# Seven block products in place of eight for the retention values and the first gate of a float32 two-layer kernel, with two of the weight sums made by adding DMAs

## The reference

```python
u = rmsnorm(h, norm_mix[l])
proj = u @ w_in[l]                                   # 1024 -> 7168
q, k, v, g_ret, p, gates = jnp.split(proj, split_points, axis=-1)
q = rotary(...); k = rotary(...) * (RET_QK_DIM ** -0.5)
ret = retention(q, k, v)                             # chunks of 64, decays
ret = ret * lax.rsqrt(jnp.mean(ret * ret, axis=-1, keepdims=True) + NORM_EPS)
ret = ret.reshape(b, s, RET_V) * jax.nn.silu(g_ret)
pool_out = multiscale_pool(p, pool_w[l], pool_scale[l])
gate = jax.nn.sigmoid(gates.reshape(b, s, 2, D_MODEL) + gate_bias[l])
merged = gate[:, :, 0] * (ret @ w_ret_up[l]) + gate[:, :, 1] * (pool_out @ w_pool_up[l])
h = h + merged @ w_out[l]
```

## Time and profile before

| | |
|---|---|
| Median of 3 runs | 1193.36 us (1192.82 to 1193.5) |
| The profiled execution's own time | 1193.28 us |
| Its span in the trace | 1191.5 us |
| PE busy | 1182.7 us, 99% of the span |
| DVE busy | 914.9 us, 77% |
| ACT busy | 674.6 us, 57% |
| POOL busy | 165.2 us, 14% |
| Granted clock of TensorE | 0.999 of full speed |

### The profile page before, as it was taken

The page is one execution under the profiler, slowest core; times in us unless marked ns, Lnnn a source line. Parts: engine busy times, 40 slices in busy tenths (PEclk is TensorE's granted clock), DMA queues, the critical chain, the costliest instruction groups (busy, mean ns, idle before and its releaser), DMA issues.

```text
span 1191.5 us, 14697 instructions
## 1 busy us (share of the span) xinstructions
PE 1182.7 (99%) x5728; PEld 982.1 (82%) x5728; DVE 914.9 (77%) x1143; ACT 674.6 (57%) x814; POOL 165.2 (14%) x169
## 2 busy tenths in 40 slices
PE   9999999999999999999999999999999999999997
PEld 8777888888888888888888888888899888888886
DVE  7788798878778798877798878645567666988884
ACT  7775656666547666554565555545333545666652
POOL 2100132210200132210132120000000000222200
PEclk9999999999999999999999999999999999999999
DMA  9434565547333565556455555745544455555540
GB/s 341 175 132 157 184 243 185 183 175 279 121 136 112 206 216 178 188 195 218 156 193 186 201 212 185 281 171 206 192 161 168 151 177 176 188 206 180 188 177 35
DMA packets 32728, 220.91 MB, mean 185 GB/s; under 512 B 3761, under 2 KB 4273, under 8 KB 7058
## 3 DMA queue, kind: packets, MB, share of 16 engines
q1 hardware_dynamic: 32514, 219.77, 51.5%
q10 hardware_dynamic: 144, 0.20, 0.0%
HBM read 218.91 MB, written 1.05 MB: 185 GB/s over the span
## 4 chain that ended last, share of the span: by engine, by line
PE 99%; issue 0%; DVE 0%; ACT 0%; POOL 0%; POOLq 0%; DVEq 0%; ACTq 0%
PE ps L259 30%; PE ps L261 30%; PE ps L260 30%; PE ps L264 5%; PE ps L267 3%; DVE h L406 0%; DVE AR L2579 0%; DVE st L1812 0%; DVE AR L1830 0%; ACT AR L2570 0%; POOLq L134 0%; POOL st L395 0%; POOL state L1546 0%; ACT yh L1862 0%; DVE st L1817 0%
## 5 line engine op out<-in xcount | busy, mean ns | idle before, releaser
L218 DVE SCALAR_TENSOR_TENSOR wlo<-raw,whi 128x2048 fp32r<-128x2048 f32 x160 | 366.3, 2294 | 114.4 <-ACT whi L211 87.1
L211 ACT CAST whi<-raw 128x2048 fp32r<-128x2048 f32 x162 | 310.0, 1914 | 193.6 <-PE ps L261 192.3
L259 PE MATMUL ps<-whi,xh 128*128 128x512 f32 x1040 | 409.9, 394 | 0.0
L261 PE MATMUL ps<-whi,xl 128*128 128x512 f32 x1040 | 405.4, 390 | 0.0
L260 PE MATMUL ps<-wlo,xh 128*128 128x512 f32 x1040 | 405.2, 390 | 0.0
L259 PEld LDWEIGHTS ps<-whi,xh 128*128 128x128 f32 x1040 | 195.2, 188 | 45.5 <-issue 1.4
L261 PEld LDWEIGHTS ps<-whi,xl 128*128 128x128 f32 x1040 | 195.2, 188 | 41.8
L260 PEld LDWEIGHTS ps<-wlo,xh 128*128 128x128 f32 x1040 | 195.4, 188 | 38.4
L259 PE MATMUL ps<-whi,yh 128*128 128x512 f32 x344 | 138.0, 401 | 0.0
L261 PE MATMUL ps<-whi,yl 128*128 128x512 f32 x344 | 134.4, 391 | 0.0
L260 PE MATMUL ps<-wlo,yh 128*128 128x512 f32 x344 | 134.0, 389 | 0.0
(11 more groups left out here) (256 smaller groups left out, 1379.8 us busy)
## 6 DMA issues: line engine op xcount, KB each, us to landing
raw<-in_w SPq DMA_DIRECT2D x198, 1024.0 KB, 4.8
raw<-in_w SPq DMA_DIRECT2D x4, 512.0 KB, 7.7
h<-in_x SPq DMA_DIRECT2D x4, 256.0 KB, 4.7
raw<-in_w SPq DMA_DIRECT2D x4, 256.0 KB, 4.3
AR<-in_b_pw SPq DMA_DIRECT2D x1, 1024.0 KB, 4.9
AR<-in_gate_bias SPq DMA_DIRECT2D x1, 1024.0 KB, 6.8
AR<-in_dft SPq DMA_DIRECT2D x1, 864.0 KB, 7.5
AR<-in_rmask SPq DMA_DIRECT2D x1, 768.0 KB, 8.7
```

Source lines behind the costliest of these rows:

```text
L211: e.copy(whi[:, v % S, :], raw[:, v % R, :]).then_inc(*sig.up("hi", v))
L218: e.scalar_tensor_tensor(out=wlo[:, v % S, :], in0=raw[:, v % R, :], scalar=1.0, in1=whi[:, v % S, :].bitcast(F32), op0=ALU.mult, op1=ALU. ...
L259: e.matmul(o, ah, bh, start=start, stop=False, skip_group_check=skip)
L261: return e.matmul(o, al, bh, start=False, stop=stop, skip_group_check=skip)
```

## The change

- v and g0 are each made by **seven block products** (`tensor_product`, p = 0 to 6) of 12 matmuls instead of eight quarters. The blocks are the two token halves, the two input halves and the two column halves. Three products (0, 2, 5) take the tokens as they are; four (1, 3, 4, 6) take one of four **token sums** (`vector_token_sums`, then a cast into `SX` on ACT and a low part `SL` on DVE, 128 x 2048 each, made once and used by both groups). Products 0, 2 and 3 take a weight block as it is (b11, b21, b22), the others a **weight sum**: product 1 takes b11 + b12, product 4 that plus b22, product 5 that plus b21, product 6 b12 + b22. Each of the seven is a unit of its own for `hi` and `lo`, so each group has seven casts and seven low parts where there were four.
- The sums for products 4 and 5 are made by DVE (`vector_group_sum`). Those for products 1 and 6 are made by **DMAs that add** (`accum_op`), issued by GpSimd: SP loads b11 into `first_sum` (the place of the token sums, so after those are read) and GpSimd adds b12 from memory to it; and GpSimd adds b22 from memory to the loaded b12 in its raw slot.
- Products share banks: 0, 4 and 6 follow each other in one (ps4), 1 and 3 in another (ps5), 2 and 5 in a third. Between them ACT copies what is there (`scalar_part`) and DVE adds to it (`vector_part`), as no matmul starts these banks anew.
- The order: the whole group v stands where v0 stood; the group g0 where v1 stood, ahead of q0. g00 and g01 are gone from behind gr1. Products ru0 follow gr1 at once, with the turns of the second retention half before and inside them. The gate's bias and sigmoid move along (`vector_gate_sum`, `scalar_gate`).
- The norm of this stage writes float32 tokens (`x32`) on ACT, then casts them (one 128 x 512 instruction) and takes the low part by one 128 x 512 instruction on DVE (before: four of 128 x 128 each).
- `vector_ret_norm` computes both token halves' sums before it scales either, in other scratch space.
- Convolution: chunk 2 has a split buffer of its own (`third`, in `SL`), and the wait is gone.

```diff
+RET = {"p0": 2, "p1": 2, "g10": 2, "g11": 2, "pw": 1, "v": 7, "pu0": 2, "pu1": 2, "g0": 7, "q0": 2, "k0": 2,
+       "q1": 2, "k1": 2, "gr0": 2, "gr1": 2, "ru0": 2, "ru1": 2, "out": 4}
+GROUPS = ("v", "g0")
+ADDED = {"v": (1, 6), "g0": (1, 6)}
+GROUP_RAW = (1, None, 2, 0, 1, 2, 3)
...
+        def raw_ready(v):
+            if v in added_at:
+                return sig.at("added%d" % (v - added_at[v]), v)
+            return sig.at("summed", v) if v in sums_at else raw_loaded(v)
+
+        def raw_free(n):
+            return lo_at(users[n][-1])
...
-                elif c == 2:
-                    q.wait_ge(*banks.filled("conv", 1, 0))
...
+        def vector_group_sum(e, q, g, k):
...
+            elif k == 4:
+                q.wait_ge(*lo_at(v))
+                q.wait_ge(*raw_loaded(v + 3))
+                q.wait_ge(*raw_ready(v + 1))
+                d = e.tensor_tensor(b11, first_sum, b22, ALU.add)
+            else:
+                q.wait_ge(*lo_at(v + 2))
+                q.wait_ge(*sig.at("summed", v + 4))
+                d = e.tensor_tensor(b21, b21, b11, ALU.add)
+            d.then_inc(*sig.up("summed", v + k))
+
+        def tensor_product(e, q, g, p):
+            bx, bz, by = GBANK[g]
+            v = RU[g] + p
+            b, key = ((bx, "x"), (bz, "z"), (by, "y0"), (bz, None), (bx, None), (by, "y1"), (bx, None))[p]
+            if key:
+                banks.take(b, g, key)
+                q.wait_ge(*banks.room(g, key))
+            else:
+                q.wait_ge(*sig.at("part", g, {3: 1, 4: 0, 6: 2}[p]))
...
+            for k in range(4):
+                c = slice(512 * k, 512 * k + 512)
+                last = mm3(e, ps[b][:, :], ah[:, k, :], al[:, k, :], whi[:, v % S, c], wlo[:, v % S, c],
+                           k == 0 and key is not None, k == 3, skip=True)
...
+        def scalar_part(e, q, g, i):
+            bx, bz, _ = GBANK[g]
+            p, b, t, j = ((0, bx, 0, 0), (1, bz, 1, 1), (4, bx, 0, 1), (6, bx, 1, 0))[i]
...
+        def vector_part(e, q, g, i):
+            bx, bz, by = GBANK[g]
+            p, b, t, j, parts = ((2, by, 0, 0, (0,)), (3, bz, 0, 1, (2,)), (6, bx, 1, 1, (1, 3)), (5, by, 1, 0, (3,)))[i]
...
@@ tensor_ret
-            chunk(e, q, "v0", RU["v0"], x)
+            for p in range(7):
+                tensor_product(e, q, "v", p)
...
-            chunk(e, q, "v1", RU["v1"], x)
+            for p in range(7):
+                tensor_product(e, q, "g0", p)
...
-            chunk(e, q, "g01", RU["g01"], x)
...
+            turn_x(e, q, "ret", None, 0, 1, vn[:, 0, :], "y", sig.at("gated", 1, 0))
+            quarter(e, q, "ru0", RU["ru0"], 0, 0, 0, yh, yl, y_ret)
+            quarter(e, q, "ru0", RU["ru0"], 0, 1, 0, yh, yl, y_ret)
+            turn_x(e, q, "ret", None, 1, 1, vn[:, 1, :], "y", sig.at("gated", 1, 1))
...
+        def gpsimd_first_sum(e, q, g):
+            v = RU[g]
+            q.wait_ge(*sig.at("ld_first", g))
+            e.dma_start(first_sum, wst[raw_of[v + 6]], accum_op=ALU.add).then_inc(*sig.up("added1", v + 1, by=16))
+
+        def gpsimd_last_sum(e, q, g):
+            v = RU[g]
+            q.wait_ge(*sig.at("added1", v + 1))
+            q.wait_ge(*raw_loaded(v + 6))
+            e.dma_start(raw_at(v + 6), wst[raw_of[v + 3]], accum_op=ALU.add).then_inc(*sig.up("added6", v + 6, by=16))
...
+                if v == raw_of[RU["v"]] - 1 and "v" in ADDED:
+                    q.wait_ge(*sig.at("x_low", "sums"))
+                    load(first_sum, wst[raw_of[RU["v"]]], "ld_first", "v")
+                if v == raw_of[RU["pu0"]] and "g0" in ADDED:
+                    q.wait_ge(*lo_at(RU["v"] + 1))
+                    q.wait_ge(*sig.at("summed", RU["v"] + 4))
+                    load(first_sum, wst[raw_of[RU["g0"]]], "ld_first", "g0")
```

More of the change, by code:

```diff
@@ L356, in norm_half_act @@
             q.wait_ge(*banks.filled("x", name, t, half))
+            if name == "nm":
+                b = banks.of["x", name, t, half]
+                q.wait_ge(*sig.at("sums", "n1", FAST - 1))
+                q.wait_ge(*sig.at("turned_lo", "n1", FAST - 1))
+                for i in range(4):
+                    k = 4 * half + i
+                    last = e.activation(x32[:, t, k, :], ps[b][:, 128 * i:128 * i + 128], ACT.Copy, bias=0.0,
+                                        scale=parm(name, k))
+                last.then_inc(*banks.empty("x", name, t, half))
+                q.wait_ge(*banks.emptied("x", name, t, half))
+                if x_free:
+                    q.wait_ge(*x_free)
+                e.copy(xh[:, 4 * half:4 * half + 4, tcols(t)],
+                       x32[:, t, 4 * half:4 * half + 4, :]).then_inc(*sig.up("xh", name, t, half))
+                return
             if x_free:
@@ L673, in vector_mix @@
             v = ff_down(U[FF[f][0]], j)
-            b11, b12, b21, b22 = (raw[:, v % R, 512 * k:512 * k + 512] for k in range(4))
+            b11, b12, b21, b22 = (raw_at(v)[:, 512 * k:512 * k + 512] for k in range(4))
             t3 = mix[:, 1, :]
-            q.wait_ge(*sig.at("raw%d" % (v % R), v))
+            q.wait_ge(*raw_ready(v))
             if j:
@@ L687, in vector_mix_rest @@
             v = ff_down(U[FF[f][0]], j)
-            b12, b21, b22 = (raw[:, v % R, 512 * k:512 * k + 512] for k in range(1, 4))
+            b12, b21, b22 = (raw_at(v)[:, 512 * k:512 * k + 512] for k in range(1, 4))
             t2, t4 = mix[:, 0, :], mix[:, 2, :]
@@ new lines, in scalar_part @@
+        def scalar_part(e, q, g, i):
+            bx, bz, _ = GBANK[g]
+            p, b, t, j = ((0, bx, 0, 0), (1, bz, 1, 1), (4, bx, 0, 1), (6, bx, 1, 0))[i]
+            q.wait_ge(*sig.at("made", g, p))
+            q.wait_ge(*sig.at("summed", "minus"))
+            q.wait_ge(*banks.filled("pooled", 3))
+            e.activation(group_dst(g, t, j), ps[b][:, :], ACT.Copy, bias=0.0,
+                         scale=(minus if j else rstd)[:, t:t + 1]).then_inc(*sig.up("part", g, i))
+        def vector_part(e, q, g, i):
+            bx, bz, by = GBANK[g]
+            p, b, t, j, parts = ((2, by, 0, 0, (0,)), (3, bz, 0, 1, (2,)), (6, bx, 1, 1, (1, 3)), (5, by, 1, 0, (3,)))[i]
+            q.wait_ge(*sig.at("made", g, p))
+            for n in parts:
+                q.wait_ge(*sig.at("part", g, n))
+            d = group_dst(g, t, j)
+            e.scalar_tensor_tensor(out=d, in0=ps[b][:, :], scalar=(minus if j else rstd)[:, t:t + 1], in1=d, op0=ALU.mult,
+                                   op1=ALU.add).then_inc(*banks.empty(g, DONE[t, j]))
@@ L2125, in vector_gate @@
             key = f"g{which}{j}"
-            dst = merged if which else sig0
+            dst = merged
             q.wait_ge(*banks.filled(key, t))
@@ L2162, in scalar_pool_out, with vector_pool_out @@
                 a.then_inc(*sig.up("pool_hi", g))
-        def vector_pool_out(e, q):
-            for g in range(4):
+        def vector_pool_out(e, q, groups):
+            for g in groups:
                 q.wait_ge(*sig.at("pool_hi", g))
@@ L2501, in vector_ret @@
             vector_ret_norm(e, q, 0)
+            for t in range(2):
+                vector_ret_scale(e, q, 0, t)
             for t in range(2):
```

352 lines of the change are left out of this document (254 added, 98 removed).

## The result

The changed kernel takes 1196.71 us (median of 7 runs, 1195.78 to 1197.29) where the kernel before takes 1193.43 (1192.82 to 1194.11): a ratio of 1.0028, 95% interval 1.0019 to 1.0037. It is slower by 3.3 us, inside the range and on the other side of no change than was forecast.

The account below looks back on a forecast made before the run. PE was taken as the bound, busy 1182.7 of 1191.5 us. Terms -5.45 - 0.2 + 0.8 + 1.7 + 0.4 = -2.75 gave a forecast of 1190.6 us, range 1189.6 to 1198.0.

Parts of the forecast that it names:

- I take 3: v's first adding DMA: chosen channel time of 3 us, from bounds 2.53 and 10; landing at 802.7, cost 0.
- W: Microsecond channel time of an adding DMA's 1 MB; 2.53 for a plain load, bounded above by 10.
- everything in v is hidden: First sum landing at 802.7, with 2.8 us to spare before 805.5, the latest landing that costs nothing: 0.
- The case of a double channel: Rival: adding DMA takes the channel twice, W about 5, landing 806.7, 1.2 late; 1193.4 us; chance 0.24.
- the two queues share by halves: Adding DMA beside SP's b11 and b21 loads: equal channel shares, giving landings from 801.8 (W = 2.5) to 813.1 (W = 10).
- that rival: GpSimd's issue held up: 2.5 us instead of 1.3, landing 803.9; 1190.6 to 1191.6 us; chance 0.05.
- The second collision: In the double-channel rival, g0's first sum delays pu0's next unit 1 to 2 us on a 0.5 margin: +1.5.
- 24 matmuls, -5.45: v and g0: 2 x 84 matmuls instead of 2 x 96, at 0.227 us each, save 5.45 us.
- Convolution, -0.2: Third cast no longer waits for PE, so PE's gap of 0.20 us goes.
- Allowance for thin margins, +0.8: Margins of 0.4 to 0.6 us at products 3, 6, pu0 and g0's counterparts may become waits; bounds 0 and 3.
- q0's bank, +1.7: Product 6 of g0 and q0 share ps4, so PE waits about 1.7 us while the bank is emptied.
- ru0, +0.4: DVE's low part stands ahead of the last turned quarter's gate product, which waits: +0.4 us, from 0 to 1.2.

Follow-up runs that it names:

- with copies: The four GpSimd-issued DMAs copy instead of adding, against the changed kernel, so the output leaves out two weight sums of each group: 1192.20 us, ratio 0.9988.
- the kernel with the other order: Against the changed kernel, SP loads b22, b11 and b21 ahead of `first_sum`: 1194.35 us, ratio 1.0005.
- The kernel with no waits left: Against the kernel whose one adding DMA is for g0's product 6, DVE makes g0's sum for product 4 right behind product 1's: 1188.75 us, ratio 0.9959.
- two other kernels: Against the changed kernel: SP loads b22, b11, b21 ahead of `first_sum` (1194.35 us); g0's products use ps2, ps5, ps3 (1194.91 us).
- the run with other banks: Against the changed kernel, g0's products use ps2, ps5 and ps3 instead of ps4, ps5 and ps2: 1194.91 us, ratio 1.0011.

## Why the prediction was wrong

**What failed is the step "I take 3" for the adding DMA's W, and with it that everything in v is hidden.** The landing was worked out as 802.7 and measured at 806.2 (issue at 793.46, 12.8 to landing); that is the value given for W between 4 and 5. By the packets an adding DMA holds all engines for 5.9 us where a copy holds them for 2.8. By the landings it takes 7.8 to 8.3 us where nothing lies beside it and a copy 5.0 to 5.2, thus 3.0 more: W = 2.5 + 3.0 = 5.5. Both put W at about twice a load. The case of a double channel (0.24) had this mechanism, and the landing within 0.5, and put the price at nothing won and nothing lost; the time came out 3.3 above it.

A second step failed with it: *that the two queues share by halves.* The table gives 801.8 for a plain 1 MB issued by 794.4; the copy, issued by 794.7, landed at 803.7. While it ran, SP's queue moved 3.1 MB beside its 1.05. That the landing at W = 5 came out right is thus in part luck. GpSimd's issue, taken as 1.3 us, was 1.05: that rival did not occur.

The adding DMA was underpriced in three ways:
- *Who is late first.* I had product 1's cast wait for the sum. The chain went through the load of b11, a plain one beside it, and product 0. By the prediction's own rule of halves it would have landed at about 799.7 (an estimate: three units of 2.53 us from 788.3, the last of them at half rate from 794.4, and the tail of 2.3); it was cast at 802.9, and at 801.5 with copies. That the loads issued behind `first_sum` inherit both SP's wait for the token sums and the sharing was in the working, but not followed to the first unit that was needed. In the kernel with the other order this alone moved the wait ahead of product 3 from 2.46 to 0.72.
- *The clock.* A wait was priced at its own length. The one of 2.46 us took 1.5 more at half clock.
- *The second collision.* Taken as 1.5 us, it was 1.4 at pu0; but the other kernels show that it can land on product 6, pu0 or pu1 with up to 3.0 and a granted clock near half behind it, by where the DMAs happen to meet.

The Trainium skill has a rule on this that the prediction didn't find: "Collectives: The Full Stack" (the section on the bandwidth ceiling) says of the reducing step of a collective that it is half as fast as the copying one, not for the addition but because it must read two sources through the same ring. The case here is another one, an addition from memory onto a tile of the core, but the 5.9 against 2.8 us of the packets agree with a factor of two. Which part reads twice no run here shows. The fit that the prediction cites from the Trainium skill ("DMA: Bandwidth & Descriptors", "Anatomy of one DMA"; 4.4 us by estimate for a plain unit) is stated there for DMAs that GpSimd issues: the copies from its queue took 5.0 to 5.2, so it was low for them too.

Point by point, as the trace and the runs have it:
- *24 matmuls, -5.45*: borne out. The kernel with no waits left, in which the slower steps named below and the work behind q0 cost some 1.5 us, ends PE's work 4.2 us earlier (1149.87 to 1145.64 for one matmul of the next stage).
- *Convolution, -0.2*: 0.25 to 0.29 in all twelve profiles with the edit, between 364 and 366. About half of it is given back at 740 to 770 (offsets of the changed kernel: -0.22 at 410, -0.12 at 740, -0.01 at 770). That is the stretch of the norm's new casts, priced at 0; no run took those alone.
- *Allowance for thin margins, +0.8*: there were waits at two of the named places, ahead of product 3 and in pu0. With copies there is still one of 0.6 to 0.8 ahead of product 3; with DVE making v's sums there is none there. The margin at product 6, where a cast that waits for a load stands ahead of `scalar_part`, was missed in two other kernels, by 2.0 and 2.2.
- *q0's bank, +1.7*: 1.80 in the trace, 1.8 by the run with other banks.
- *ru0, +0.4*: the stretch from q0 to the end costs +0.7 against before. The wait itself is where it was forecast and has its size: PE waits for a turned low part at 963.4 (one step of 0.45), behind a low part of weights on DVE, and these 24 matmuls take 5.96 us where the 24 from 978.03 on take 5.56. Of the other 0.3, some 0.1 arises under q and k and 0.2 behind 980; no run took them apart.
- *The step of a product's matmul.* Not in the sum: 84 matmuls of a group take 19.47 and 19.41 us in the kernel without waits, 0.231 a step in the mean and not 0.227. Twice 0.4 us. Most of it is in the products that take token sums, with 0.233 a step; those that take the tokens as they are have 0.227 to 0.231. The cause was not tried.

With W = 2.5 the sum would have come nearer: the copies gave 1192.2 for 1190.6. The slower step (0.8) and the other 0.3 behind q0 lie between, and 0.5 that stays open.

## What to carry to other kernels

A DMA that adds is not a load with an addition for free: price it at twice the load's channel time, and then ask which plain loads lie beside it, for here one of them was late before the sum was. Where a queue gets a wait in its middle, follow everything issued behind it to the first consumer; here three loads whose slots were free stood behind it. And if an engine has idle time at the right place, let it do the sum and put it into a wait that is there anyway: that, with other banks for g0, turned +3.3 us into -4.6.

## What was not expected of the hardware

- An adding DMA of 1 MB lands 7.8 to 8.3 us after its issue alone, 8.1 to 9.1 with little beside it, 9.3 to 13.3 among loads; a copy from the same queue 5.0 to 5.2, and 9.7 among loads. Alone, its packets hold the 16 engines for 5.6 to 6.0 us, a copy's for 2.8 to 3.0. The plain load of b11 took 13.7 beside the adding DMA and 11.7 beside the copy, third in its queue both times, where one alone takes 4.8.
- Some kernels scatter: 1191.2 to 1197.7 and 1190.2 to 1196.0 with adding DMAs and SP's other order, where the kernel before keeps within 1.5 us but for two runs and the one with a single adding DMA and no wait within 0.5. The addition alone does not account for it: with DVE making all sums the runs go from 1192.6 to 1195.5, and the changed kernel itself keeps within 1.5.
- TensorE's granted clock was down (0.51 to 0.63 in the 3 to 4 us behind) after waits of 2.00, 2.11, 2.22, 2.46 to 2.49 (three profiles) and 2.99 us. It stayed full after those of 1.35, 1.44 and 1.80, and once after one of 2.21. Where it fell in the changed kernel it cost 1.5 us more than the wait itself.
- The matmuls of the products that take token sums run at a step of 0.233 us. Those that take the tokens as they are keep the 0.227 that the same form had in v0, but for their first few.
